# High and low parts of two neighbouring expert tiles in one instruction, from tile 38 on

## The reference, cut to what matters

```python
def block(xb):
    qb = (xb @ w_q).reshape(TOKEN_BLOCK, PEER_HEADS, 2, PEER_DKEY)
    s = jnp.einsum('thcd,hcnd->thcn', qb, sub_keys)
    s_top, i_top = lax.top_k(s, PEER_TOPK)
    cand = s_top[:, :, 0, :, None] + s_top[:, :, 1, None, :]
    cand_idx = i_top[:, :, 0, :, None] * PEER_NKEYS + i_top[:, :, 1, None, :]
    ...
    best, pos = lax.top_k(cand, PEER_TOPK)
    eidx = jnp.take_along_axis(cand_idx, pos, axis=-1)
    g = jax.nn.softmax(best, axis=-1)
    ug = jnp.take(u, eidx, axis=0)
    vg = jnp.take(v, eidx, axis=0)
    h = jax.nn.gelu(jnp.einsum('td,thkd->thk', xb, ug), approximate=False)
    return jnp.einsum('thk,thkd->td', (g * h).astype(x.dtype), vg)
```

## Time and profile before

| | |
|---|---|
| median of three runs | 1654.39 us (1652.92 to 1654.4) |
| span of the profiled execution | 1652.1 us |
| PE busy | 1634.0 us, 99% |
| DVE busy | 1246.6 us, 75% |
| ACT busy | 646.1 us, 39% |
| POOL busy | 464.2 us, 28% |

### The profile page before, as it was taken

The page is one execution under the profiler, slowest core; times in us unless marked ns, Lnnn a source line. Parts: engine busy times, 40 slices in busy tenths (PEclk is TensorE's granted clock), DMA queues, the critical chain, the costliest instruction groups (busy, mean ns, idle before and its releaser), DMA issues.

```text
span 1652.1 us, 23515 instructions
## 1 busy us (share of the span) xinstructions
PE 1634.0 (99%) x9093; PEld 1456.3 (88%) x9093; DVE 1246.6 (75%) x2357; ACT 646.1 (39%) x1006; POOL 464.2 (28%) x218
## 2 busy tenths in 40 slices
PE   9999999999999999999999999999999999999997
PEld 7898987888888999999999999999998888888886
DVE  3023456444799999998888789998998888888887
ACT  5333345543222343345545333333333433333332
POOL 4432223343224557410000223333333122222100
PEclk9999999999999999999999999999999999999999
DMA  5431112126112558588787999999999999999961
GB/s 204 157 140 52 52 54 77 45 83 230 52 52 82 182 176 295 190 330 279 242 281 237 350 390 394 380 388 370 358 375 375 390 384 375 375 363 386 399 242 70
DMA packets 135135, 407.05 MB, mean 246 GB/s; under 512 B 10352, under 2 KB 71024, under 8 KB 113776
## 3 DMA queue, kind: packets, MB, share of 16 engines
q1 hardware_dynamic: 116592, 271.32, 45.1%
q0 software_dynamic: 18432, 134.23, 20.7%
HBM read 360.94 MB, written 44.56 MB: 245 GB/s over the span
## 4 chain that ended last, share of the span: by engine, by line
PE 81%; DVE 17%; DMA 1%; issue 1%; ACT 0%; DVEq 0%; SPq 0%
PE bank L1303 24%; PE bank L1305 24%; PE bank L1304 24%; PE bank L1585 3%; PE bank L1422 2%; DVE idx L1084 1%; DVE idx L1076 1%; DVE val L1075 1%; DVE val L1083 1%; DVE tmp L1077 1%; PE bank L1437 1%; DVE prod L1140 1%; PE bank L1393 1%; PE bank L1385 1%; DVE prod L1149 1%
## 5 line engine op out<-in xcount | busy, mean ns | idle before, releaser
L1303 PE MATMUL bank<-xhi,whi 128*128 128x384 f32 (+1 forms) x1408 | 499.5, 355 | 2.3 <-ACT hout L824 1.8
L1305 PE MATMUL bank<-xhi,wlo 128*128 128x384 f32 (+1 forms) x1408 | 492.7, 350 | 0.0
L1304 PE MATMUL bank<-xlo,whi 128*128 128x384 f32 (+1 forms) x1408 | 492.0, 349 | 0.0
L629 POOL DMA_INDIRECT uvb<-in_uv,eidx x128 | 201.6, 1575 | 697.8 <-DVE acc L1191 667.4
L803 ACT ACTIVATE whi<-raw 128x1024 fp32r<-128x1024 f32 x256 | 270.2, 1057 | 254.4 <-PE bank L1305 228.1
L1169 DVE TENSOR_TENSOR wlo<-raw,whi 128x1024 fp32r<-128x1024 f32 x218 | 265.9, 1221 | 78.9 <-ACT whi L803 78.2
L1305 PE MATMUL bank<-whi,alo 128*128 128x512 f32 x768 | 299.5, 390 | 0.0
L1304 PE MATMUL bank<-wlo,ahi 128*128 128x512 f32 x768 | 299.4, 390 | 0.0
L1303 PE MATMUL bank<-whi,ahi 128*128 128x512 f32 x768 | 298.7, 389 | 0.0
L1303 PEld LDWEIGHTS bank<-xhi,whi 128*128 128x128 f32 x1408 | 264.5, 188 | 18.8 <-issue 3.9
L1305 PEld LDWEIGHTS bank<-xhi,wlo 128*128 128x128 f32 x1408 | 264.3, 188 | 15.6
(11 more groups left out here) (202 smaller groups left out, 1848.2 us busy)
## 6 DMA issues: line engine op xcount, KB each, us to landing
raw<-in_u SPq DMA_DIRECT2D x128, 512.0 KB
raw<-in_uv SPq DMA_DIRECT2D x128, 512.0 KB
g_scratch<-stage SPq DMA_DIRECT2D x48, 512.0 KB, 5.1
gl<-g_scratch SPq DMA_DIRECT2D x32, 768.0 KB
raw<-in_w_in SPq DMA_DIRECT2D x22, 1024.0 KB, 4.8
h_scratch<-hout SPq DMA_DIRECT2D x88, 192.0 KB, 5.3
hl<-h_scratch SPq DMA_DIRECT2D x22, 768.0 KB, 10.1
raw<-in_w_q SPq DMA_DIRECT2D x6, 1024.0 KB, 4.7
```

The lines of the kernel that those rows point to most:

```text
L629: nc.gpsimd.indirect_dma_start(out=uvb[:, k % UVB, :], out_offset=None, in_=a["uv"][:, :], in_offset=bass.IndirectOffsetOnAxis(ap=eidx[:, ...
L1303: mm(out, lh, rh, start=first, stop=False)
L1304: mm(out, lh, rl, start=False, stop=False)
L1305: return mm(out, ll, rh, start=False, stop=last)
```

## The change

Up to tile 37 nothing is different. From tile 38 on, ACT makes the high parts of tiles s + 3 and s + 4 in one instruction of 2048 columns at odd steps s, and none at even steps. DVE makes the low parts of tiles s and s + 1 in one instruction at even steps s, and none at odd steps. The semaphores rise by two. All else stands as it was.

```diff
+            def pair_high(n):
+
+                for i in (n, n + 1):
+                    act.wait_ge(traw[i % 4], 16 * (i // 4 + 1))
+                two = slice(slot4(n), slot4(n) + 2)
+                nc.scalar.activation(whi4[:, two, :], raw4[:, two, :], ACT.Copy).then_inc(tile_hi, 2)
+
...
-                tile_high(s + 4)
+                if s + 4 < POOL_ONLY:
+                    tile_high(s + 4)
+                elif s % 2 == 1 and s + 3 >= POOL_ONLY:
+                    pair_high(s + 3)
                 for q in quads_after(s):
                     g_evac(q)
...
-            def tile_low(n):
-
-                dve.wait_ge(tile_hi, n + 1)
-                V.tensor_tensor(wlo4[:, slot4(n), :], raw4[:, slot4(n), :], whi4[:, slot4(n), :].bitcast(F32),
-                                ALU.subtract).then_inc(low_dve, 1)
+            def pair_low(n):
+
+                dve.wait_ge(tile_hi, n + 2)
+                two = slice(slot4(n), slot4(n) + 2)
+                V.tensor_tensor(wlo4[:, two, :], raw4[:, two, :], whi4[:, two, :].bitcast(F32),
+                                ALU.subtract).then_inc(low_dve, 2)
...
-                if s >= POOL_ONLY:
-                    tile_low(s)
+                if s >= POOL_ONLY and s % 2 == 0:
+                    pair_low(s)
```

## The result

The changed kernel takes 1807.72 us, the median of four runs (1802.42 to 1812.2), beside 1654.06 us for the kernel before: ratio 1.0931, 95% interval 1.091 to 1.0953. The direction is that of the forecast, the size is not: 154 us in place of 84, and outside the range. The profiled execution took 1802.42 us with a span of 1800.6; 1800.6 - 1652.1 = 148.5 us is what the traces have to account for.

What follows compares the result with a forecast made beforehand. The prediction took PE, busy 1634 of 1652 us, as the bound, so only its new waits count. Terms of 44, 11.5, 4 and 25 us made 84.5 on 1654.4, so 1738 us, range 1700 to 1772.

Steps and rivals of the forecast that it cites:

- What bounds the kernel, what is saved: Whole kernel: PE bounds it; 23 us of ACT and 16 us of DVE are saved, 0 us on the path.
- Term 1: Steps 46 to 81: even steps' one-hots come late behind the wide low part, PE waits; 44 us with the start.
- The sum: Whole kernel: the four terms add 84.5 us to the median, so 1738 us.
- transfers are worse: Rival, chance 0.13: v-tile loads at their upper bound or beyond, or PE's clock falls to 1.2 GHz; 1775 us and more.
- The start: Pair of tile 46: DVE about 4 us late for the first two one-hot batches; 4.0 us, within term 1.
- Term 2: Steps 89 to 106, u tiles to alternating ones: late gelu of a u tile and less room; 11.5 us.
- Term 3: Rest of the alternating part, to step 168: less room for low parts, mostly hidden; 4 us, bounds 0 and 12.
- Term 4: V tiles from step 168: load of tile s + 5 queues behind gl and hl, in a ring; 25 us, bounds 0 and 45.
- if ACT waits for PE there as today, term 4 is wrong: Sign for the v tiles: ACT's high part should wait for raw in every second pair, not for PE.
- The end: Norms of the last tokens: forecast as unchanged, with no loss in the sum.

Runs made afterwards that it cites:

- e4: Changed kernel, but in odd steps ACT makes the high part of the activations behind the wide high part, not ahead of it; 1766.53 us.
- e11: Changed kernel with one-hots ahead of low parts, high part of activations behind the wide high part, both loads ahead of gl and hl; 1677.53 us.
- e8: Changed kernel with two narrow instructions in place of each wide one, same places, on ACT and DVE, a semaphore count for each tile; 1733.7 us.

## Why the prediction was off

**What bounds the kernel, what is saved.** Right: none of the saved DVE and ACT time is seen at the end in any run, and what counted were waits of PE, with what they brought along.

**Term 1, the one-hots: mechanism right, a part of the price left out.** Forecast 40.0 us from step 46 to 81, measured 62.7. The waits were forecast as 2.2, 1.3 and 3.8 us and are 2.24, 1.32 and 3.27; their sum is 37.4, with one of 0.7 for ACT 38.1, for 40.0. The step that failed is "2.2 us of wait" taken as 2.2 us of loss. The sum priced each wait by its own length, at the full clock; the fall of the clock stood in the rival "transfers are worse" with the sentence that waits of up to 1.5 us had left it at 2.4 GHz (true, though the earlier trace rows begin 280 us behind these waits). The new waits are longer and come 2.5 to 15 us apart, and cost another 21.2 us by the clock, over half of their own length, and 3.4 us with 0.15 us for each. With the waits filled by matmuls the same stretch lost 43.8, near the forecast's 40.0: the sum was right for a clock that stays up. The start (steps to 46) was 6.9 for 4.0: the two waits there grew from 2.0 to 5.1 us, PE waited 1.2 us for a gelu, and 6.8 us at 1.2 GHz followed.

**Term 2, the turn: right within its bounds, 8.4 for 11.5.** PE waited 1.80 us for the gelu of a u tile (for 4 forecast) and 2.57 once for a low part:

```profile
1039.74 0.41 PE L1314 MATMUL bank<-xhi,whi 128*128 128x384 f32 x1 [1.80 <-ACT hout L831]
...
1059.13 0.44 PE L1314 MATMUL bank<-xhi,whi 128*128 128x384 f32 x1 [2.57 <-DVE wlo L1180]
```

**Term 3: within its bounds, 10.0 for 4.** 5.5 us had come by step 160, and 4.5 came in the eight steps from there to 168.

**Term 4, the v tiles: the mechanism that decided was missing, 53.7 for 25.** The forecast had the ring of low part, product, gl, hl and raw tile, and left out a shorter one that was in the diff and in the order of the code: ACT's pair_high of an odd step stands behind high_a of the step before it, which waits for DVE's product. Before the change that did no harm, since ACT made single high parts one tile ahead; with one wide high part for two tiles, made in the step in which it is wanted next, both engines stand in line. The line "if ACT waits for PE there as today, term 4 is wrong" was the right question with one answer too few: ACT waits for the loads only 4.1 us and once 5.9, and for DVE 169.2 and 89.8. That it was this order, e4 shows with 33 us at the v tiles. The forecast mechanism was not imaginary: it struck once, at tile 171, whose load landed 17 us after its issue behind gl and hl; for the rest it lay behind the other, and came up once that was removed, with 20 us in e11.

**The end.** The sum had nothing for it; 6.9 us are lost from step 252 on. PE waits 5.0 of them for low parts of activations (0.85 us ahead of tile 253 and 4.13 ahead of 254), and behind the longer wait it ran at 1.2 GHz once more.

**The sum.** 6.9 + 62.7 + 8.4 + 10.0 + 53.7 + 6.9 = 148.6, for 84.5 forecast. The misses are 21 us of clock at the one-hots and 3 that go with the waits, 29 us at the v tiles, 7 at the end, 6 in term 3 and 3 at the start, less 5 us of waits and turn that came out smaller. The rival "worse" (1775 us and more, chance 0.13) was the case that came, by one of its two mechanisms and one that was not thought of; that its time covered 1807 us is in part luck. Its price could have been read ahead: with waits in two of three pairs longer than any that the trace of before had shown harmless, the fall of the clock deserved to be in the sum.

**What stays open.** e8 has as many waits at the one-hots as the changed kernel, 22, and the clock costs some 1.6 us there in place of 21.2: their number alone does not bring it down. Whether the length of the single wait does it or the sum of neighbouring ones was not separated. The 12 us beside PE's waits at the v tiles were not taken apart. Why the last stretch costs 6.9 us in the changed kernel and 2.0 to 4.2 in those with mended orders was not tried by itself.

## What to carry to other kernels

A wide instruction on a feeding engine saves its fixed cost only if that engine is the limit; otherwise look at what it takes away, which is the hand-over piece by piece, and at everything that stands behind it in the order and is wanted sooner. Follow each in-order engine once around: if its next product stands behind a wait for the engine that waits for this product, the two run in turn, and the length of that ring against the bound's own pace is the loss. Where a busy TensorE gets new waits of 2 us every few tiles, price them above their own length, and remember that a limit removed shows the one behind it: the same edit of the loads was worth 13 us and then 20.

## What the runs showed of the hardware that was not expected

22 waits of 0.7 to 2.6 us, 38.1 us in 257, took the granted clock of TensorE from 1.00 to a mean of 0.90, and this cost 21.2 us. Behind each of the 11 waits of 2.2 us and more it ran at 1.2 GHz for a while, behind the six of 1.32 us it never did. The same 22 waits cut to at most 1.5 us (25.4 us together) brought it down once. Matmuls of no use in the waits made the kernel faster by 22 us, 1785.6 for 1807.7.
